# Attention divisions on GpSimd, one head's eviction on VectorE, and a reordered third norm

## What is computed

```python
# layer 1, attention: 16 heads of 64
s = concat([q . k_window + bias, q . k_context])
p = softmax(s)
o = p[:n] @ v_window + p[n:] @ v_context
h = h + g1 * (o @ w_out)
# layer 1, FFN: the third norm is the rms_norm here
u = rms_norm(h, norm_ffn_w) * (1 + sc2) + sh2
a, g = split(u @ w_up)
h = h + g2 * ((gelu(conv3(a) + conv_b) * g) @ w_down)
return rms_norm(h, final_norm_w)
```

## Time and profile before

| | us |
|---|---|
| median of 3 runs | 1783.93 |
| lowest, highest | 1783.24, 1788.70 |
| the profiled execution | 1782.06 |
| its span, first to last instruction | 1780.2 |
| TensorE busy in it | 1709.4 (96%) |
| VectorE, ScalarE, GpSimd busy | 924.7, 755.4, 543.3 |
| attention's transposes, first to last | 1247.7 to 1342.3 |
| third norm, first late sums to last low part | 1381.3 to 1415.4 |

### The profile page before, as it was taken

One profiled execution on the slowest core, in us unless ns is written; L12 is line 12 of the kernel. 1 busy time (PEld: TensorE's weight loads), 2 busy tenths in 40 slices (PEclk: granted clock), 3 DMA queues, 4 the chain that ended last, 5 costly groups with the idle time before them and its releaser, 6 DMA issues.

```text
span 1780.2 us, 26540 instructions
## 1 busy us (share of the span) xinstructions
PE 1709.4 (96%) x9744; PEld 1484.1 (83%) x9744; DVE 924.7 (52%) x1468; ACT 755.4 (42%) x1208; POOL 543.3 (31%) x249
## 2 busy tenths in 40 slices
PE   5999899997999999999999999999999899999997
PEld 2777788896899999999988888997668888888876
DVE  5777966667956566566523365001774532222344
ACT  3563434776332332323333445212884443334442
POOL 1122113553222332233222323322004234444442
PEclk9999999998999999999999999999999999999998
DMA  8323223443432433433321122121322123222221
GB/s 335 138 95 119 73 72 100 138 132 130 142 119 96 141 130 107 142 121 116 100 67 60 60 72 84 60 95 59 105 74 83 60 82 96 95 95 96 94 95 59
DMA packets 66588, 184.08 MB, mean 103 GB/s; under 512 B 5920, under 2 KB 26784, under 8 KB 65200
## 3 DMA queue, kind: packets, MB, share of 16 engines
q1 hardware_dynamic: 44784, 164.69, 27.4%
q10 hardware_dynamic: 21696, 17.88, 3.4%
HBM read 180.40 MB, written 2.15 MB: 103 GB/s over the span
## 4 chain that ended last, share of the span: by engine, by line
PE 80%; DVE 5%; ACT 2%; issue 1%; POOL 0%; ACTq 0%; DVEq 0%; POOLq 0%
PE ps L2363 28%; PE ps L2789 13%; PE ps L2362 13%; PE ps L2376 4%; PE ps L2443 3%; PE ps L2786 3%; PE ps L2721 2%; PE ps L2923 2%; PE ps L2902 2%; PE ps L2936 2%; PE ps L2449 1%; PE ps L2346 1%; PE ps L2456 1%; PE ps L2345 1%; PE ps L2636 1%
## 5 line engine op out<-in xcount | busy, mean ns | idle before, releaser
L692 POOL TENSOR_TENSOR wsp<-raw,wsp 128x1024 fp32r<-128x1024 f32 x185 | 457.0, 2470 | 1133.5 <-ACT wsp L763 1133.1
L763 ACT ACTIVATE wsp<-raw 128x1024 fp32r<-128x1024 f32 x185 | 196.3, 1061 | 453.1 <-PE ps L2363 350.5
L2362 PE MATMUL ps<-v_a,wsp 128*128 128x384 f32 x1008 | 342.7, 340 | 0.0
L2363 PE MATMUL ps<-v_b,wsp 128*128 128x386 f32 x1008 | 340.2, 337 | 0.0
L2789 PE MATMUL ps<-hsp,wsp 128*128 128x512 f32 x984 | 277.4, 393 | 2.5 <-DVE hsp L2009 2.5
L2789 PEld LDWEIGHTS ps<-hsp,wsp 128*128 128x128 f32 x984 | 183.6, 188 | 45.3 <-issue 4.4
L2363 PE MATMUL ps<-uf,wsp 128*128 128x512 f32 x888 | 201.4, 389 | 0.0
L2363 PEld LDWEIGHTS ps<-uf,wsp 128*128 128x128 f32 x888 | 166.7, 188 | 34.6
L2363 PEld LDWEIGHTS ps<-v_b,wsp 128*128 128x128 f32 x1008 | 193.5, 192 | 0.0
L2362 PEld LDWEIGHTS ps<-v_a,wsp 128*128 128x128 f32 x1008 | 189.2, 188 | 0.0
L2026 DVE SCALAR_TENSOR_TENSOR conv<-apad,vec,conv 128x770 f32<-128x770 f32 (+1 forms) x44 | 47.6, 1082 | 204.2 <-ACT conv L1201 204.2
(11 more groups left out here) (320 smaller groups left out, 2537.2 us busy)
## 6 DMA issues: line engine op xcount, KB each, us to landing
raw<-in_weights SPq DMA_DIRECT2D x281, 512.0 KB, 3.8
nab<-in_nabias ACTq DMA_DIRECT2D x32, 256.0 KB, 3.0
start_w<-in_start SPq DMA_DIRECT2D x6, 1024.0 KB, 20.9
h<-in_x SPq DMA_DIRECT2D x4, 768.0 KB, 14.5
mD<-rows_scratch ACTq DMA_DIRECT2D x12, 256.0 KB, 4.1
mqs<-rows_scratch ACTq DMA_DIRECT2D x12, 256.0 KB, 5.3
h<-in_x ACTq DMA_DIRECT2D x2, 1536.0 KB, 6.4
start_w<-in_start SPq DMA_DIRECT2D x4, 512.0 KB, 12.5
```

Source lines behind the costliest of these rows:

```text
L692: pool.tensor_tensor(w[:, 1, :], raw[:, raw_index(s) % 4, :], w[:, 0, :].bitcast(F32), ALU.subtract)\
L763: act.activation(split_of(s)[:, 0, :], raw[:, raw_s % 4, :], ACT.Copy).then_inc(*own.one(hi_ready))
L2362: pe.matmul(cx, w, x_cx[:, k, xp, :], start=first, stop=last)
L2363: mm = pe.matmul(lat, w, x_lat[:, k, xp, :], start=first, stop=last)
```

## The change

GpSimd now does the two multiplications by the reciprocals of each pair. VectorE takes the reciprocals as before and signals them on a new semaphore `na_dve`. VectorE also evicts the odd head's transposes (`turned_out`), and ScalarE only the even head's. The order on VectorE in turn p becomes biased(p), the reciprocals of p - 1, turned_out(p - 2). TensorE waits for either engine's eviction in `turn` and for both in `values`. On GpSimd the divisions stand between the weight blocks S_OUT1 and S_OUT1 + 2.

In the third norm, rows 6 and 7 of the second half are added at k = 3 and k = 5 of the first half's `half_operand`, ScalarE squares them at those places, and TensorE's late sums for the second half stand behind k = 4, not k = 2.

`hsp` begins 256 bytes lower.

```diff
-        hsp = at("hsp", [P, 2, 2, N_TOK], f0 + 18944, F32R)
+        hsp = at("hsp", [P, 2, 2, N_TOK], f0 + 18688, F32R)
...
+        def rec_count(p):
+            return p + 1 if p < 2 else 2 * p
+
+        def pt_count(p):
+            return 2 * p + 3 if p < N_NA - 2 else N_NA + p + 1
...  (GpSimd)
+            def divide(p):
+                x = 2 * p % NA_SLOTS
+                pool.wait_ge(na_dve.sem, rec_count(p))
+                for y in range(x, x + 2):
+                    pool.tensor_scalar(nas[:, y, :], nas[:, y, :], nast[:, y, 2:3], None, ALU.mult)\
+                        .then_inc(*own.one(p_ready))
...
             for s0 in S_RINGS:
+                if s0 > S_OUT1:
+                    blocks(own.loop, {lo_ready: 4}, S_OUT1 + 1 - begin, lambda n, i: low(begin + n, i))
+                    divide(0)
+                    low(S_OUT1 + 1, 0)
+                    for p in range(1, N_NA):
+                        divide(p)
+                    begin = S_OUT1 + 2
...  (ScalarE)
-                    for e in range(2 * p - 4, 2 * p - 2):
-                        act.wait_ge(p_turned.sem, e + 1)
-                        act.activation(nap[:, g % 2, e % 2, :, p % 2, :],
-                                       ps[:, 4 + e % 2, :].rearrange("p (a b) -> p a b", a=4), ACT.Copy)\
-                           .then_inc(*own.one(pt_ready))
+                    act.wait_ge(p_turned.sem, 2 * p - 3)
+                    act.activation(nap[:, g % 2, 0, :, p % 2, :], ps[:, 4, :].rearrange("p (a b) -> p a b", a=4), ACT.Copy)\
+                       .then_inc(*own.one(pt_ready))
...
-                    if k == 4:
-                        half_square(q, f, 1, 6)
-                half_square(q, f, 1, 7)
+                    if k in (3, 5):
+                        half_square(q, f, 1, 6 if k == 3 else 7)
...  (VectorE)
-                    if ends is not None and k in (4, KT):
-                        ends(6 if k == 4 else 7)
+                    if ends is not None and k in (3, 5):
+                        ends(6 if k == 3 else 7)
...
-                dve.reciprocal(nast[:, x:x + 2, 2], nast[:, x:x + 2, 1]).then_inc(*own.one(dve_own))
-                dve.wait_ge(*own.last())
-                for y in range(x, x + 2):
-                    dve.tensor_scalar(nas[:, y, :], nas[:, y, :], nast[:, y, 2:3], None, ALU.mult)\
-                       .then_inc(*own.one(p_ready))
+                dve.reciprocal(nast[:, x:x + 2, 2], nast[:, x:x + 2, 1]).then_inc(*own.one(na_dve))
+
+            def turned_out(p):
+                g = p // 2
+                if g >= 2:
+                    dve.wait_ge(o_done.sem, g - 1)
+                dve.wait_ge(p_turned.sem, 2 * p + 2)
+                dve.tensor_copy(nap[:, g % 2, 1, :, p % 2, :], ps[:, 5, :].rearrange("p (a b) -> p a b", a=4))\
+                   .then_inc(*own.one(na_dve))
...
+                if 2 <= p < N_NA + 2:
+                    turned_out(p - 2)
...  (TensorE)
-                            if half == 0 and pair[0] == 0 and k == 2:
+                            if half == 0 and pair[0] == 0 and k == 4:
                                 late_sums(n, 4, 6, 9, KT + M_LATE)
...
-                    if e >= 2:
-                        pe.wait_ge(pt_ready.sem, e - 1)
+                    if p:
+                        pe.wait_ge(*((na_dve.sem, pt_count(p - 1)) if e % 2 else (pt_ready.sem, p)))
...
-                pe.wait_ge(pt_ready.sem, 4 * g + 4)
+                pe.wait_ge(pt_ready.sem, 2 * g + 2)
+                pe.wait_ge(na_dve.sem, pt_count(2 * g + 1))
```

More of the change, by code:

```diff
@@ L325, in build @@
         gel = at("gel", [P, 2, CW], f0 + 12352)
-        hsp = at("hsp", [P, 2, 2, N_TOK], f0 + 18944, F32R)
-        assert f0 + 18944 + 4 * T <= AR_END
+        hsp = at("hsp", [P, 2, 2, N_TOK], f0 + 18688, F32R)
+        assert f0 + 18688 + 4 * T <= AR_END
         naq = at("naq", [P, KT, N_LAT], ar)
@@ L364, in build @@
         g_lo_late = sem("g_lo_late")
+        na_dve = sem("na_dve")
+        def rec_count(p):
+            return p + 1 if p < 2 else 2 * p
+        def pt_count(p):
+            return 2 * p + 3 if p < N_NA - 2 else N_NA + p + 1
         act_own, dve_own, pool_own = map(sem, ("act_own", "dve_own", "pool_own"))
@@ L2203, in divided @@
                 dve.wait_ge(p_exp.sem, 2 * p + 2)
-                dve.reciprocal(nast[:, x:x + 2, 2], nast[:, x:x + 2, 1]).then_inc(*own.one(dve_own))
-                dve.wait_ge(*own.last())
-                for y in range(x, x + 2):
-                    dve.tensor_scalar(nas[:, y, :], nas[:, y, :], nast[:, y, 2:3], None, ALU.mult)\
-                       .then_inc(*own.one(p_ready))
+                dve.reciprocal(nast[:, x:x + 2, 2], nast[:, x:x + 2, 1]).then_inc(*own.one(na_dve))
+                assert na_dve.k == rec_count(p)
+            def turned_out(p):
[5 more added lines that the diff above has]
+                   .then_inc(*own.one(na_dve))
+                assert na_dve.k == pt_count(p)
             for cg in range(2):
```

## The result

The changed kernel takes 1826.88 us (median of 4 runs, 1826.51 to 1827.63), against 1783.7 for the kernel before (4 runs): a ratio of 1.0242, 95% interval 1.0229 to 1.0256. It is 43 us slower. The forecast was 1787.5 with a range of 1780 to 1798, and no rival reached further than 1804.8.

The account below looks back on a forecast made before the run. TensorE, busy 96% of the span, was taken as the bound. Divisions +9.3, norm -5.7, rows 0 gave +3.6 us on the profiled 1782.06: 1785.7, or 1787.5 as a median, that execution lying 1.9 under; range 1780 to 1798.

Parts of the forecast that it names:

- What bounds attention: Attention's steady state: TensorE busy 6.12 of 6.15 us a period; the division is the last link, without cover.
- 6.15 + 2D - 0.90: Attention's period of two pairs in us after the change; 0.58 us lost a period, 16 times, +9.3 us.
- D: One GpSimd division of 128x512 in attention: estimated 0.74 us, floor 0.57, ceiling 1.28.
- Rival (a): GpSimd's division slower because writes take turns with reads: 0.93 us, +9.7 us, 1793.6; at 1.28, 1804.8; chance 0.39.
- Rival (b): GpSimd's division at the floor of 0.57 us, the memset's pace: -1.9 us, 1782.0; chance 0.20.
- The chain's small terms: Attention's division chain: handovers 0.10 us to GpSimd and 0.14 to TensorE, 0.53 for the second head's transposes and change to values.
- In the other turn the values' 1.88 us cover a D up to about 1.4: Attention's turn with values between: GpSimd divisions up to about 1.4 us each are hidden there.
- VectorE's eviction at nothing: VectorE's new 0.69 us PSUM copy in attention costs nothing; without the values' cover 0.15 us a period, 2.4 us.
- No contention added: In attention VectorE reads PSUM and at most one SBUF tile, so nothing was added for contention with GpSimd.
- The norm: Third norm: late sums at 1396.45, not 1399.24, spread near 1400.1, not 1405.96, clock staying up; -5.7 us.
- Rival (d): The clock falls in the third norm all the same: norm gains 4.0, sum +5.3 us, 1789.2; chance 0.06.
- The rows: Rows 256 bytes lower, read by the second layer's down phase: 0 us, with 1.7 us allowed in the range.

Follow-up runs that it names:

- experiment 10: The changed kernel with 4 and 3 identity matmuls, useless for the result, filling TensorE's waits ahead of the even and odd heads' transposes: 1814.81 us, ratio 1.0165.
- experiment 5: The kernel before with only the divisions moved to GpSimd, both evictions on ScalarE, norm and rows as before: 1836.22 us against 1785.19, ratio 1.0279.
- experiment 12: The changed kernel with GpSimd dividing only the odd head of each pair and VectorE the even one: 1794.63 us, ratio 1.005.
- experiment 2: The kernel before with only the third norm's reordering, the down rows left where they were: 1777.69 us, ratio 0.9968.

## Why the prediction was wrong

**What bounds attention.** Right. TensorE sets the period, the division is the last link and has no cover; the waits that appeared are exactly those. The formula 6.15 + 2D - 0.90 held within 0.06 us at four values of D.

**The term that was mis-sized is D.** The prediction took 0.74 us from a pace of a two-input row halved, with the two-input row of 1.28 as the ceiling. It measured 1.56. The failing step was the ceiling's premise, that an operation with one tensor in can't be slower than one with two. The rows of before had a two-input operation, a wide memset and a copy of 4 elements, and no `tensor_scalar` on GpSimd at all. A row of another opcode bounds nothing from above. Rival (a) had the right direction and deciding point (D from 0.79 on), and was cut off at the same false ceiling. Its mechanism isn't borne out: if reads and writes took turns, the copy, one stream in and one out, would take the 0.93 us that (a) worked out, and it takes 0.613. The forecast's own picture, inputs one after the other, fails too: three operations with one tile in take 0.61, 1.49 and 1.56 us. The duration goes with the operation, and why `tensor_scalar` is so slow stays open.

At D = 1.56 the prediction's own sum is 16 x 2.23 - 5.7 = +29.9 us. The kernel of experiment 10, in which the clock stays up, is 29.6 us above its kernel before.

The Trainium skill (GPSIMD Engine Reference, section Engine selection) calls a one-input elementwise operation on GpSimd roughly line-rate. For the copy the run comes near that: 0.613 us, beside the 0.57 worked out at the memset's pace. For `tensor_scalar` the runs speak against it, 1.49 us with a constant, and the measurement decides. Rival (b), at the floor, had a chance of 0.20 and gave 1782.0.

**The chain's small terms.** Their sum was right, in part by luck. The prediction had 0.14 us from GpSimd to TensorE and 0.53 for the second head's transposes. In the changed kernel's period from 1299.90 us, GpSimd's second division ends at 1303.00, the transposes start at 1303.06 and the values at 1303.65: 0.06 and 0.59, and the two errors cancel.

**The term that was missing is the clock in attention.** 15.8 us. The prediction saw in the norm that the clock falls when TensorE idles and priced it there, but not in the stage where it was itself adding idle time. At D = 0.74 this would have been right: up to D = 1.04 the clock stayed at 1.00, and at D = 1.49 and 1.56 it fell in more than half of the periods. Such a cost doesn't grow in proportion to D.

**"In the other turn the values' 1.88 us cover a D up to about 1.4".** At 1.56 this cover is a little short. The periods lie on the formula without it (8.39 against 8.38), so it cost at most some hundredths of a us; nothing isolates it.

**VectorE's eviction at nothing.** Right in the changed kernel (experiment 5). Where the divisions stay on VectorE the copy costs 0.63 us a period. The prediction's "0.15 without cover" was the wait of the bias. The wait that came was TensorE's for the bank.

**No contention added.** Right for the changed kernel: D is the same to 9 ns over 64 divisions, with VectorE reading PSUM beside it. It holds only because VectorE's divisions went. In experiment 12 one of them came back and GpSimd slowed by 0.29 us.

**The norm.** Right: 5.8 us for the spread was forecast, 24.65 - 18.89 = 5.76 measured. The sums were forecast 1396.45 - 1381.31 = 15.14 us behind the first half's, and came 1447.47 - 1432.33 = 15.14 behind them. The clock stayed up. Rival (d) didn't happen.

**The rows.** Right, 0 (experiment 2). For the 1.7 us that the range allows for them the prediction had no row, and no run shows such an effect: the down product's matmuls take 277.3 and 277.4 us.

**The range.** It took its upper end from D = 1.05, on the strength of a ceiling that was argued and not measured. 16 periods times 2D makes each 0.1 us of D 3.2 us of time. With no row of the operation in the trace, the range had to allow for a D well above the nearest neighbour.

## What to carry to other kernels

When work is moved to GpSimd, look for a row of the same opcode there, or measure one. A form with fewer inputs isn't a cheaper form: here a product by a per-row factor takes 1.56 us as `tensor_scalar`, 1.04 as `tensor_tensor` with a broadcast. Then ask where the moved step's input becomes ready and what stands ahead of that on its queue. Swapping two calls on VectorE took away some 40 us, while the slow operation stayed. The two remedies together, the two-input form and the early reciprocal, weren't run. And where a change adds idle time to TensorE in a loop, price the clock as a cost of its own. A probe for it is to fill the idle time with matmuls that fit in it: 4 and 3 of them told here, 8 and 6 were too many.

## What the runs showed of the hardware that was not expected

- GpSimd, 128x512 in float32: copy 0.61 us, two inputs with one broadcast 1.04, two full tiles 1.28, `tensor_scalar` with a constant 1.49, with a pointer 1.56.
- TensorE's clock went down to 1.2 GHz in attention after idle stretches of 1.16 and 0.89 us a period (a granted clock of 0.52 in the values, 0.83 in the mean over a period), and the values that followed took 3.63 us in the place of 1.95. It stayed at 2.4 GHz when matmuls without use filled those stretches. Why some periods of the same kernel are spared (the one from 1261.5 us, and the three from 1330.0 to 1355.2 with the same idle stretches) wasn't found out.
- GpSimd's `tensor_scalar` took 1.857 us beside VectorE's `tensor_scalar` from SBUF to SBUF and 1.563 without it, while VectorE's took 0.486 and, before, 0.483. VectorE loses nothing, GpSimd 0.29 us. The Trainium skill (SBUF — State Buffer, section Who interferes with whom) names this form among those in which VectorE can take the port pair that it shares with GpSimd, and says that whoever comes later is blocked. The traces agree with it in direction, VectorE's being the first by 0.06 us. In size GpSimd loses 0.29 us, less than the 0.43 that VectorE's has left when GpSimd's starts. VectorE's copies from PSUM beside the same division did nothing to it.
